# 48 modulation blocks of the first layer taken from TensorE: scaled by ScalarE, added up by GpSimd, summed over rows by TensorE once a piece

## What is computed

```python
c_act = jax.nn.silu(c)
for l in range(DEPTH):
    mod = c_act @ w_ada[l] + b_ada[l]
    shift, scale, gate = jnp.split(mod, 3, axis=-1)
    h = _rmsnorm(x, norm_g[l]) * (1.0 + scale[:, None, :]) + shift[:, None, :]
    z = h @ w_in[l]
    ...
    y = jnp.concatenate([o_fft, o_na, o_ret, o_cv], axis=-1) @ w_out[l]
    x = x + gate[:, None, :] * y
```

## Time and profile before

| | |
|---|---|
| runs | 2183.64, 2188.57, 2193.8 us, median 2188.57 us |
| profiled execution, first to last instruction | 2186.2 us |
| mean granted clock of TensorE | 0.991 of full speed |
| busy: PE, PEld, DVE, ACT, POOL | 2116.0, 1783.3, 1473.3, 950.6, 201.7 us |
| moved by DMA | 512 MB, 234 GB/s |
| loads into `ada_raw` and `ada_fourth` from GpSimd's queue | 272 and 48, 512 KB each |

### The profile page before, as it was taken

One profiled execution on the slowest core, in us unless ns is written; L12 is line 12 of the kernel. 1 busy time (PEld: TensorE's weight loads), 2 busy tenths in 40 slices (PEclk: granted clock), 3 DMA queues, 4 the chain that ended last, 5 costly groups with the idle time before them and its releaser, 6 DMA issues.

```text
span 2186.2 us, 32887 instructions
## 1 busy us (share of the span) xinstructions
PE 2116.0 (97%) x13626; PEld 1783.3 (82%) x13626; DVE 1473.3 (67%) x1873; ACT 950.6 (43%) x1326; POOL 201.7 (9%) x386
## 2 busy tenths in 40 slices
PE   5889999999999999999999999999999999999997
PEld 3668878987889879977887878787778999988876
DVE  0355879876856888855896665659686787455554
ACT  2235555553535645546632222223346444444453
POOL 2211110110010111010010000001100001000000
PEclk9989999999999999999999999999999999999999
DMA  9998887789697777787585555545885778322253
GB/s 380 372 328 303 281 314 242 249 276 328 211 353 269 255 270 255 251 305 258 196 286 177 179 167 164 173 154 177 301 293 158 243 254 299 101 75 75 87 184 134
DMA packets 215597, 512.45 MB, mean 234 GB/s; under 512 B 19728, under 2 KB 26080, under 8 KB 213664
## 3 DMA queue, kind: packets, MB, share of 16 engines
q1 hardware_dynamic: 155536, 297.83, 40.2%
q0 software_dynamic: 54576, 202.79, 26.8%
q10 hardware_dynamic: 5344, 9.84, 1.4%
HBM read 501.97 MB, written 8.43 MB: 233 GB/s over the span
## 4 chain that ended last, share of the span: by engine, by line
PE 68%; DVE 8%; DMA 4%; ACT 2%; issue 2%; DVEq 0%; ACTq 0%
PE ps L806 20%; PE ps L807 19%; PE ps L808 19%; DMA w_raw<-in_w_out 2%; DVE ada_acc L2286 2%; PE ps L862 2%; DVE wl L2386 1%; PE ps L1480 1%; DMA ada_raw<-in_ada_w 1%; DVE wl L2393 1%; PE ps L1217 1%; PE ps L1183 1%; PE ps L1472 1%; PE ps L1463 1%; ACT wh L1584 0%
## 5 line engine op out<-in xcount | busy, mean ns | idle before, releaser
L2393 DVE TENSOR_TENSOR wl<-w_raw,wh 128x1024 fp32r<-128x1024 f32 x280 | 334.6, 1221 | 198.7 <-ACT wh L1584 197.3
L1584 ACT ACTIVATE wh<-w_raw 128x1024 fp32r<-128x1024 f32 x280 | 291.6, 1056 | 347.9 <-PE ps L808 239.5
L1636 ACT ACTIVATE wh<-w_raw 128x1024 fp32r<-128x1024 f32 x220 | 230.9, 1058 | 418.5 <-PE ps L808 361.6
L2386 DVE TENSOR_TENSOR wl<-w_raw,wh 128x1024 fp32r<-128x1024 f32 x220 | 266.4, 1220 | 173.9 <-ACT wh L1636 173.6
L806 PE MATMUL ps<-hh,wh 128*128 128x256 f32 x1280 | 371.7, 290 | 10.4 <-DVE hl L2454 9.7
L807 PE MATMUL ps<-hh,wl 128*128 128x256 f32 x1280 | 361.5, 282 | 0.0
L808 PE MATMUL ps<-hl,wh 128*128 128x256 f32 x1280 | 360.9, 282 | 0.0
L2286 DVE SCALAR_TENSOR_TENSOR ada_acc<-ada_raw,cpad,ada_acc 128x1024 f32<-128x1024 f32 x263 | 329.5, 1280 | 15.4 <-DMA ada_raw<-in_ada_w 13.3
L806 PEld LDWEIGHTS ps<-hh,wh 128*128 128x128 f32 x1280 | 242.9, 190 | 36.9 <-issue 22.9
L806 PE MATMUL ps<-wh,act_hl 128*128 128x512 f32 x640 | 256.1, 400 | 1.1 <-DVE wl L2386 1.0
L807 PE MATMUL ps<-wh,act_hl 128*128 128x512 f32 x640 | 253.3, 396 | 0.0
(11 more groups left out here) (401 smaller groups left out, 3265.0 us busy)
## 6 DMA issues: line engine op xcount, KB each, us to landing
ada_raw<-in_ada_w POOLq DMA_DIRECT2D x272, 512.0 KB, 5.2
w_raw<-in_w_in SPq DMA_DIRECT2D x208, 512.0 KB, 5.5
w_raw<-in_pool_in SPq DMA_DIRECT2D x72, 512.0 KB, 4.7
w_raw<-in_w_out SPq DMA_DIRECT2D x64, 512.0 KB, 7.9
w_raw<-in_mla_in SPq DMA_DIRECT2D x56, 512.0 KB, 4.7
ada_fourth<-in_ada_w POOLq DMA_DIRECT2D x48, 512.0 KB, 6.6
w_raw<-in_pool_out SPq DMA_DIRECT2D x48, 512.0 KB, 5.2
w_raw<-in_mla_out SPq DMA_DIRECT2D x32, 512.0 KB, 4.2
```

The costliest lines, as they stand in the source:

```text
L1584: act.activation(wh[:, g % RING, :], w_raw[:, g % RING, :], ACT.Copy).then_inc(w_hi, 1)
L1636: act.activation(as_raw(g, wh[:, r, :]), raw_of(g), ACT.Copy).then_inc(w_hi, 1)
L2386: dve.tensor_tensor(as_raw(g, wl[:, r, :]), raw_of(g), as_raw(g, wh[:, r, :].bitcast(F32)), ALU.subtract).then_inc(w_lo, 1)
L2393: dve.tensor_tensor(wl[:, g % RING, :], w_raw[:, g % RING, :], wh[:, g % RING, :].bitcast(F32), ALU.subtract).then_inc(w_lo, 1)
```

## The change

Pieces 2, 4 and 5 of layer 0 move from `ADA_PE` to a new table `ADA_POOL`, in the same steps and numbers. For such a block

- ScalarE multiplies it in place with its factors, behind the mixers of the block's step;
- GpSimd adds it to `pool_acc`, 128 x 1024 values that lie in the buffer `hc` (the first block of a piece is copied). `ada_block(q - 2)` stands in GpSimd's queue behind the load of block q;
- a buffer is free when GpSimd has added its block (`ada_pooled`);
- in the step of `ADA_FIN`, ahead of its mixers, TensorE sums `pool_acc` over rows, as it does for VectorE's pieces, and waits for GpSimd's last addition; the next piece's copy waits for this sum.

Layer 1 keeps its tables. Besides, two semaphores are given up to make room: `t_dg` is replaced by a further count of `t_gp`, and `p_sc2` by the chained wait `link`; the instructions there are the same.

```diff
-ADA_PE = [{**spread(2, 4, [1, 2, 2, 2, 3, 3, 3]), **spread(4, 12, [4] + [3] * 4), **spread(5, 19, [2] * 8)},
+ADA_POOL = [{**spread(2, 4, [1, 2, 2, 2, 3, 3, 3]), **spread(4, 12, [4] + [3] * 4), **spread(5, 19, [2] * 8)}, {}]
+ADA_PE = [{},
...
+ADA_POOLED = [(2, 4, 5), ()]
...
+            def ada_freed(q):
+
+                by, n = ADA_SEQ[q][4:]
+                pool.wait_ge((ada_used, ada_pe, ada_pooled)[by], n + ADA_RING if by == BY_DVE else n)
+
+            def ada_block(q):
+
+                layer, _, j, k, by, n = ADA_SEQ[q]
+                if by != BY_POOL:
+                    return
+                buf = ada_buf(q % ADA_RING_A)
+                pool.wait_ge(ada_scaled, n)
+                if k == 0:
+                    before = ADA_POOLED[layer].index(j)
+                    if before:
+                        t = next(t for t, i in ADA_FIN[layer].items() if i == ADA_POOLED[layer][before - 1])
+                        pool.wait_ge(ada_pe, ADA_DONE[layer, t])
+                    ins = pool.tensor_copy(pool_acc, buf)
+                else:
+                    pool.wait_ge(ada_pooled, n - 1)
+                    ins = pool.tensor_tensor(pool_acc, pool_acc, buf, ALU.add)
+                ins.then_inc(ada_pooled, 1)
+
             def ada_load(q, l, piece, k):
 
                 if q >= ADA_RING_A:
-                    by_pe, n = ADA_SEQ[q - ADA_RING_A][4:]
-                    pool.wait_ge(ada_pe if by_pe else ada_used, n if by_pe else n + ADA_RING)
+                    ada_freed(q - ADA_RING_A)
                 pool.dma_start(ada_buf(q % ADA_RING_A), ada_v[:, l * KT + k, piece * ADA_W:(piece + 1) * ADA_W]
                                ).then_inc(ada_here(q)[0], 16)
+                if q >= 2:
+                    ada_block(q - 2)
...
+                    if t in ADA_FIN[l] and ADA_FIN[l][t] in ADA_POOLED[l]:
+                        j = ADA_FIN[l][t]
+                        pe.wait_ge(ada_pooled, max(x[5] for x in ADA_SEQ if x[4] == BY_POOL and x[:3:2] == (l, j)))
+                        pe.wait_ge(ada_read, ada_event(l, t))
+                        ada_sum(None, 0, ADA_FIN_BANKS[l][t])
...
                     mixers(t)
+                    for q, (layer, step, j, k, by, _) in enumerate(ADA_SEQ):
+                        if by == BY_POOL and (layer, step) == (l, t):
+                            act.wait_ge(*ada_here(q))
+                            buf = ada_buf(q % ADA_RING_A)
+                            act.activation(buf, buf, ACT.Copy, scale=csil(0, k)).then_inc(ada_scaled, 1)
```

More of the change, by code:

```diff
@@ L99, in spread @@
     return out
+BY_DVE, BY_PE, BY_POOL = range(3)
 ADA_DVE = [{**spread(0, 0, [1] * 8 + [2, 1, 2, 1, 2]), **spread(1, 13, [1, 2, 1, 2, 2, 2] + [1] * 6),
@@ L145 @@
 assert len(ADA_SEQ) % ADA_RING_A == 0
-DVE_LAYERS = sum(not x[4] for x in ADA_SEQ)
+DVE_LAYERS = sum(x[4] == BY_DVE for x in ADA_SEQ)
 def ada_event(l, t):
@@ L220 @@
 PE_SUM = {16: 1, 17: 2, 18: 3, 19: 4, 20: 5, 21: 6 + ADA_SLOTS - LAST_DVE}
-ADA_PE_LAYERS = max(x[5] for x in ADA_SEQ if x[4])
+ADA_PE_LAYERS = max(x[5] for x in ADA_SEQ if x[4] == BY_PE)
 def both_vectors(n):
@@ L452, in program @@
         ht = ptr
+        pool_acc = hc[:, :, :].rearrange("p a n -> p (a n)")
         gate_rows = (dec[:, :], ptr[:, 0, :])
@@ L569, in program @@
             sem("p_" + n) for n in ("u", "ps", "hi", "lo", "gate", "grp", "ohi", "olo", "y", "sc"))
-        t_gp, t_dg, t_ps, t_row, t_x, t_mul, t_add = (
-            sem("t_" + n) for n in ("gp", "dg", "ps", "row", "x", "mul", "add"))
+        t_gp, t_ps, t_row, t_x, t_mul, t_add = (
+            sem("t_" + n) for n in ("gp", "ps", "row", "x", "mul", "add"))
         tabs_in = sem("tabs_in")
@@ L1062, in ada_middle @@
                         ada_turn(ada_event(l, t), ADA_FIN_BANKS[l][t])
-                    here = sum(x[4] and x[0:2] == (l, t) for x in ADA_SEQ)
+                    here = sum(x[4] == BY_PE and x[0:2] == (l, t) for x in ADA_SEQ)
                     seen = 0
-                    for q, (layer, step, j, k, by_pe, _) in enumerate(ADA_SEQ):
-                        if by_pe and (layer, step) == (l, t):
+                    for q, (layer, step, j, k, by, _) in enumerate(ADA_SEQ):
+                        if by == BY_PE and (layer, step) == (l, t):
                             seen += 1
@@ L2635, in ada_in_layer @@
                 def ada_in_layer(t):
-                    for q, (layer, step, j, k, by_pe, n) in enumerate(ADA_SEQ):
-                        if not by_pe and (layer, step) == (l, t):
+                    for q, (layer, step, j, k, by, n) in enumerate(ADA_SEQ):
+                        if by == BY_DVE and (layer, step) == (l, t):
                             if k:
```

32 lines of the change are left out of this document (17 added, 15 removed).

## The result

The change makes the kernel slower: 2258.76 us (median of 4 runs, 2252.7 to 2263.72) against 2188.28 us, a ratio of 1.031 (95% interval 1.029 to 1.033). The forecast had the sign, but 2216 us for the time, and a range that ended at 2250: the loss is 70 us, not 30.

The account below looks back on a forecast made before the run. TensorE, 97% busy, bounds the kernel now; after the change VectorE bounds steps 10 to 26. Steps 4 to 9 give -5 us, steps 10 to 26 +34, one row sum +1: +30 on 2186.2, 2216 us, range 2168 to 2250.

Parts of the forecast that it names:

- What leaves TensorE: Steps 4 to 26, first layer: 48 blocks leave TensorE, 29.9 us; three row sums add 2.4, leaving 27.5 us.
- stage two: Steps 10 to 26, 219 to 465 us: VectorE becomes the bound, 280.2 us for 246.0, +34 us.
- stage one: Steps 4 to 9, 145 to 219 us: 8.2 us less of TensorE, 5 counted, so -5 us.
- What comes to ScalarE: 48 passes, +50.7 us busy; late landings in long steps 8, 10, 12, 14, 16; step 12's conversion 5.5 us late.
- What comes to GpSimd: Steps 4 to 26: 45 additions and 3 copies at 2.0 us each, 96 us, not a bound.
- VectorE beside a reading GpSimd: Steps 10 to 26: 35 additions hold VectorE up 85% of their 2.0 us, 59.5 us more.
- The row sums: Heads of steps 11 and 17: TensorE's waits for GpSimd's last addition fall into ScalarE's delay, counted once.
- The sum: Whole span: stage one -5, stage two +34, one row sum +1, making +30 us on 2186.2; chance 0.50.
- 8 + 4: Steps 10 to 26, added to VectorE's time: four late conversions at 2 us each, and 4 us of waits that stay.
- Rival 1: Steps 4 to 26: TensorE stays the bound, additions cost VectorE nothing, loads arrive in time; 2159 us, chance 0.14.
- Rival 2: Steps 4 to 26: additions do not hold VectorE up, but ScalarE comes late; 2184 us, chance 0.24.
- Rival 3: Steps 4 to 26: GpSimd gives way, additions last some 4 us longer, VectorE loses nothing; 2204 us, chance 0.12.

Follow-up runs that it names:

- e11: Kernel before without the 48 blocks' passes and additions and with convolution taps cut to 64 positions: 2162.2 us, 26.2 less than the kernel before with the same short taps.
- e4: The change with neither ScalarE's passes nor GpSimd's additions, blocks loaded but unused: 2171.3 us, ratio 0.993 to the kernel before.
- e3: The change without GpSimd's additions and copies, ScalarE's 48 passes kept: 2185.9 us, ratio 0.999 to the kernel before.
- e1: The change with GpSimd's additions and copies replaced by fills, which write but do not read: 2212.3 us, ratio 1.011 to the kernel before.
- e5: The change with each GpSimd addition replaced by a copy, one operand read: 2214.8 us, ratio 1.012 to the kernel before.
- e12: The change with GpSimd's additions over 512 values in place of 1024: 2222.8 us, ratio 1.015 to the kernel before.
- e14: e3 with GpSimd waiting, ahead of block q's load, until ScalarE has passed block q - 3: 2197.2 us, ratio 1.003 to the kernel before.
- e2: The change without ScalarE's 48 passes, GpSimd adding blocks unscaled as they land: 2235.3 us, ratio 1.022 to the kernel before.
- e13: e3 with GpSimd filling its accumulator behind each load without waiting for ScalarE: 2190.8 us, ratio 1.000 to the kernel before.

## Why the prediction was wrong in size, step by step

- **What leaves TensorE.** 29.9 us by distances between starts, 27.5 with the sums: right as an amount of TensorE's time, 26.2 us in e11. As a gain it is 17.3 us (e4). The forecast did not need it in stage two, and the 5 us that it counted in stage one are right taken alone: e4's stage one is 5.2 us shorter.
- **What comes to ScalarE.** 1.056 us for a pass; the trace has 1.14. Waits for landings came where they were named, 4.2 us in step 12 (forecast 267.1 - 260.5 = 6.6), and 36.7 of 41.8 us in the five long steps. What they cost was put too low: 8 us in stage two, nothing of its own in stage one. The passes alone cost 9.9 and 8.3 us (e3 against e4).
- **What comes to GpSimd.** 2.0 us for an addition was too little: 2.34 us at least, 2.41 and 2.54 us in the median. The estimate of 2.25 us from the Trainium skill (GPSIMD Engine Reference, § 3.1 Elementwise — side-by-side cycle accounting) was nearer.
- **VectorE beside a reading GpSimd.** The mechanism that carried the forecast is shown (e1 to e5). In stage two VectorE's busy time grew by 71.3 us where 59.5 stood, because the additions are longer: 91.5 us of GpSimd's time in place of 70. The share of it that reaches VectorE is 0.78 in stage two, and over both stages 85.7 of 121 us, 0.71 and not 0.85. Taking VectorE's busy share for it was a guess that came near; what the traces show is a nearly fixed part of each instruction that does not reach VectorE (e5, e12). The rule of the Trainium skill (SBUF — State Buffer, § Who interferes with whom), that a VectorE instruction with two SBUF inputs contends with a GpSimd instruction that reads SBUF and not with one that only writes, agrees with e1: 1.219 us beside fills, 1.59 beside additions.
- **The row sums.** "They fall into the same delay" holds for step 17; in step 11 up to 3.1 us do not.
- **The sum.** Here the prediction failed, in two terms: VectorE's idle time in stage two, and what passes and additions cost in stage one. In stage two, 12 us of idle time were left to VectorE ("8 + 4"), and 24.2 stayed. The missing 12 us are no lateness of passes: with neither passes nor additions (e4) stage two already holds 25.2 us of VectorE's idle time beside 208.6 us of its work, and what the additions lengthened came on top of both, nearly one for one. In stage one "VectorE's 34 us of slack cover 13 additions" and nothing for the passes made -5 us; it became 10.1 us longer. Against e4 the additions alone cost 7.7 us there, the passes alone 8.3, both 15.4. With both VectorE is still idle for 37.2 us while it is busy 10.7 us longer. My reading, which no run isolates: idle time of an engine that is one link in a chain (ScalarE, VectorE, TensorE and back through four ring places) lies where the chain makes it wait, the additions where blocks are ready, so it covers them only in part. Of the 39 us that the stages went beyond the forecast (68 against 29), stage one is 15, VectorE's busy time in stage two 12, its idle time there 12.
- **The rivals.** Rival 1 needs additions that cost VectorE nothing; they cost 86 us. Rival 2 at 2184 us was off too: with VectorE's two-operand instructions at their old durations e1 is at 2212, and the queue's wait alone costs 9 of that (e14). Rival 3 happened once in 48 (below).
- **The range** took 2250 us from full turns and three passes in stage two, but kept -5 us for stage one and the small idle time in both cases. The terms were widened one by one and the frame that added them was not.

No run here is faster than the kernel before by moving blocks in a form that computes them. e3 and e4 bound what another way of adding could win: 3 us with ScalarE's passes, 17 us without.

## What to carry to other kernels

Before giving GpSimd elementwise work beside a busy VectorE, count what VectorE does in that stretch: if it is mostly instructions with two SBUF inputs, take GpSimd's whole time, less some 0.6 us for each instruction (0.54 to 0.73 here), as time added to VectorE, however free both engines look. Whether the kernel gets longer by as much depends on the stretch: here nearly all of it did in stage two, less than half in stage one (e2 against e4). A wait put into a queue that also issues loads costs by itself, 9 us here for 48 waits without any work. And test the worth of the saving first, with the work simply left out; here that one run would have said 17 us where the costs were 87.

## What the runs showed of the hardware that was not expected

- Fills do hold VectorE up in one form. In e1 three of VectorE's one-operand instructions from SBUF to SBUF (TENSOR_SCALAR) are lengthened, by 3.1 us in all, one of them from 0.75 to 2.33 us, and no two-operand instruction is; in e13 fills lengthen two such instructions, by 1.5 us. Reading additions do it too: of the 44 lengthened instructions of the change two are of this kind (0.75 to 2.90 us at 514.3 us, 0.41 to 2.37 at 244.4), the other 42 have two operands.
- GpSimd can be the one that waits. 13 additions take 2.67 to 2.89 us where the shortest take 2.34; in 12 of them an instruction of VectorE had 0.42 to 0.64 us left to run as the addition started. And one addition, at 329.76 us, takes 7.12 us in place of 2.4. It comes at the moment when VectorE starts the four low halves of step 15, and these keep their 1.22 us. The timelines of GpSimd and VectorE of after:

```profile
329.76 7.12 POOL L768 TENSOR_TENSOR hc<-hc,ada_raw 128x1024 f32<-128x1024 f32 x1 [1.64 <-ACT ada_raw L1911]
...
330.00 4.61 DVE L2434 TENSOR_TENSOR wl<-w_raw,wh 128x1024 fp32r<-128x1024 f32 x4
334.54 3.42 DVE L2327 SCALAR_TENSOR_TENSOR ada_acc<-ada_raw,cpad,ada_acc 128x1024 f32<-128x1024 f32 x1
```

  The addition starts 0.24 us ahead of the low halves, while the taps' last instruction still runs (it ends at 330.1), and is done only at 336.9. The four low halves take 4.61 us together, as without an addition beside them. Then VectorE's own modulation block takes 3.42 us in place of 1.28. So VectorE can hold GpSimd off over several instructions; it did in one of 48 cases. Why in this one and not in the others, no run tells.
